# A hybrid decoder trunk on one core: order of work and of loads in the opening, and in group 2 of the second mixer

## The chip, the core and the metric

One core of a Trainium2 chip runs the whole program in one launch. The metric is the device time of that core in microseconds (us); lower is better. In the text PE is TensorE (matmuls; PEld its weight loads), DVE is VectorE, ACT is ScalarE, POOL is GpSimd, SP is SyncE, which here only issues loads. An engine runs its own instructions in order; engines wait for one another by semaphores.

## The reference

The trunk has two layers. Layer 0 is half-step SwiGLU, a GLA mixer, half-step SwiGLU; layer 1 is the same around a Mamba-2 (SSD) mixer. The input is 256 tokens of 1024 values in float32.

```python
def swiglu(h, w_gate, w_up, w_down):
    return (silu(h @ w_gate) * (h @ w_up)) @ w_down       # 1024 -> 2816 -> 1024

def ssd_mixer(h, ...):                                     # 8 groups of 256 channels
    z, xbc, dt = split(h @ w_in)
    xbc = silu(causal_conv4(xbc) + conv_b)                 # 4 taps along time
    xs, bm, cm = split(xbc)
    ... # chunked scan: scores cm.bm with decays, state carried over chunks, + d_skip * xs
    y = y * silu(z); y = rmsnorm over each group's 256 channels
    return y @ w_out

for i in range(2):
    x = x + 0.5 * rmsnorm(swiglu(rmsnorm(x, g[0]), ...), g[1])
    x = x + rmsnorm(mixer_i(rmsnorm(x, g[2])), g[3])
    x = x + 0.5 * rmsnorm(swiglu(rmsnorm(x, g[4]), ...), g[5])
```

## The kernel before

**Precision.** Each weight tile and each activation is split in two parts in float32r: a high part (a rounded copy) and a low part (the value minus the high part). Each product is three matmuls: high-high, high-low, low-high. So each weight tile that a load brings into `raw` costs ACT a copy (the high part, `hi` L538, or `gate_up_hi` L610 for a quarter of a gate and up pair) and DVE a subtraction (the low part, `lo` L1017, `gate_up_lo` L1099). PE waits for the low part. There are four weight slots in `raw` and `ws`: 0 and 1 hold gate and up of a unit in a SwiGLU, 2 and 3 hold two down tiles. In a mixer slot 0 is P1, 1 is P2, 2 is P3 and 3 is O (a quarter of the output weights, "out").

**A SwiGLU** runs over 11 units of 256 hidden columns, `u` = 0 to 10. For a unit PE sweeps over gate and up (48 matmuls of 512 columns, L1560, in four quarters by weight rows; a "half" of a unit's load is two quarters of both matrices). ACT takes silu of gate (`gate`, L615), DVE multiplies by up (`hidden`, L1105), PE transposes (`hidden_T`, L1571), ACT and DVE split the transposed values (`hT_high` L620, `hT_low` L1112), and PE multiplies them with the down tile (24 matmuls, L1581) after the next unit's sweep. In PE's order unit u's sweep is followed by the first half of down u-1 (12 matmuls), the transposes of unit u, the second half of down u-1, then the sweep of u+1. The code for one unit on ACT and on DVE is `body` in `ffn`. It begins with the high or low part of the down tile, then the next unit's first quarters, then silu or product of this unit.

**The opening** is the first SwiGLU's start. Unit 0's weights come in four quarter loads of each matrix, then SP issues unit 1 (two halves), down 0, down 1, unit 2 (two halves), down 2, and in a loop down u and unit u. A half of a unit's load waits until the low parts that free its place are made (`gu_lo`). POOL issues small parameter loads and the load of a row of gains for the first residual update (512 KB in the buffer `gpost`).

**The second mixer** (`ssd`) runs over 8 groups `g`, as a software pipeline: in step g PE projects group g (P1 gives x, P2 gives B and C, P3 gives z; 48 matmuls of 256 columns each), scans group g-1 and adds group g-2's output with quarter g-2 of the output weights. On DVE a group's projections pass `convolution(g, 0)` for x and `convolution(g, 2)` for B and C (each 2 tensor_scalar L1287 and 6 scalar_tensor_tensor L1290 of 256 columns), and a scanned group passes `norm` (some 13 operations on 2 columns, then two on 256 columns, L1374, which give `yn`). PE transposes x of group g-1 (`rows`, L1849) and `yn` of group g-2 (`transpose_rows`, L1839), and forms `scores` (L1858, L1861). ACT copies projections out of PSUM (`tiles_out`, L556), makes silu of z (`gate_silu`, L836), of the convolved features (`feature`, L842), the squares for the norm, and the transposed output (`transposed`, L877). POOL makes three scaled copies of the transposed x (`side_products`: `xw`, `xdt`, `dx`, L491, L494, L499), issues the spread of decay rows into `exps` and masks them (`causal`, L477). Steps 3 to 6 are one loop; steps 1, 2, 7 and later are written apart, with flags `first` (g is 1), `second` (g is 2), `ahead` (7) and `tail` (8).

## Time and profile before

| | us |
|---|---|
| median of 3 runs | 1115.28 (1114.52 to 1117.74) |
| the profiled execution, its own time | 1114.35 |
| its span in the profile, first to last instruction | 1112.6 |
| PE busy | 1094.2 (98%) |
| DVE, ACT, POOL busy | 727.4, 637.1, 54.9 |
| mean granted TensorE clock | 0.998 of full speed |

PE is busy nearly all the time, so time can come back only where it stands still or runs at a lower clock. In the timeline a row gives start, length, engine, line, operation, tiles and, in brackets, the idle time before it with the engine that ended it. Some rows merge several instructions (x2, x6): the length is then from the first start to the last end.

### The profile page before, as it was taken

What the parts mean: (1) busy time and instruction counts of PE and PEld (TensorE: products, weight loads), DVE (VectorE), ACT (ScalarE), POOL (GpSimd) and SP (SyncE); (2) the same over time, 40 slices, a digit from 0 to 9 for tenths busy, and PEclk for the clock granted to TensorE, in tenths of its full rate; (3) what the DMA queues carried; (4) which work ended last, traced back from release to release, by engine and by line L of the source; (5) the groups of instructions that cost most, each with busy time, mean ns of one, the idle gap of its engine ahead of it and who ended that gap; (6) DMA issues with size and microseconds to landing.
All of it is one profiled execution on the core that took longest, in us unless ns stands there. A gap on an engine that the chain in (4) does not pass through costs nothing.

```text
span 1112.6 us, 16272 instructions
## 1 busy us (share of the span) xinstructions
PE 1094.2 (98%) x5821; PEld 932.5 (84%) x5821; DVE 727.4 (65%) x1158; ACT 637.1 (57%) x994; POOL 54.9 (5%) x81
## 2 busy tenths in 40 slices
PE   9999999999999999999999999999999999999997
PEld 7788888899878888888888887899999977888886
DVE  5655555796686555558555546789999988545553
ACT  7544445685575444457544445686777787544443
POOL 3000000000000000000000000142111110000000
PEclk9999999999999999999999999999999999999999
DMA  9955653475357655554756546276544526656531
GB/s 276 319 167 179 211 166 115 132 228 176 128 154 246 224 167 173 181 196 157 239 169 210 185 125 200 88 237 224 174 151 151 165 107 223 228 168 223 164 102 38
DMA packets 162878, 199.26 MB, mean 179 GB/s; under 512 B 6372, under 2 KB 145856, under 8 KB 162832
## 3 DMA queue, kind: packets, MB, share of 16 engines
q1 hardware_dynamic: 160288, 190.86, 52.9%
q0 software_dynamic: 2384, 7.72, 2.2%
q8 instruction: 27, 0.44, 0.2%
q14 instruction: 19, 0.16, 0.0%
q10 hardware_dynamic: 160, 0.08, 0.0%
HBM read 197.56 MB, written 1.08 MB: 179 GB/s over the span
## 4 chain that ended last, share of the span: by engine, by line
PE 90%; DVE 5%; DMA 2%; ACT 2%; issue 1%; SPq 1%; DVEq 0%; ACTq 0%
PE ps L1560 42%; PE ps L1581 25%; PE ps L1616 10%; PE ps L1626 6%; PE ps L1571 2%; DMA raw<-in_ffn_w_down 1%; PE ps L1961 1%; DVE ws L1099 1%; DVE ws L1017 1%; DVE xres L1065 1%; DMA raw<-in_ffn_w_up 1%; PE ps L1733 1%; PE ps L1604 0%; ACT ws L538 0%; DVE xT L1089 0%
## 5 line engine op out<-in xcount | busy, mean ns | idle before, releaser
L1560 PE MATMUL ps<-ws,xT 128*128 128x512 f32 x2208 | 513.5, 390 | 2.7 <-DVE xT L1089 2.2
L1560 PEld LDWEIGHTS ps<-ws,xT 128*128 128x128 f32 x2208 | 412.0, 188 | 92.7 <-issue 4.8
L1581 PE MATMUL ps<-ws,hT 128*128 128x512 f32 x1344 | 330.7, 396 | 0.0
L1099 DVE TENSOR_TENSOR ws<-raw,ws 128x1024 fp32r<-128x1024 f32 x184 | 223.4, 1223 | 120.6 <-ACT ws L610 120.6
L1581 PEld LDWEIGHTS ps<-ws,hT 128*128 128x128 f32 x1344 | 248.5, 189 | 52.4 <-issue 2.0
L610 ACT ACTIVATE ws<-raw 128x1024 fp32r<-128x1024 f32 x184 | 193.2, 1061 | 151.0 <-PE ps L1560 143.3
L1017 DVE TENSOR_TENSOR ws<-raw,ws 128x2048 fp32r<-128x2048 f32 (+1 forms) x87 | 197.5, 2271 | 84.3 <-ACT ws L538 84.0
L538 ACT ACTIVATE ws<-raw 128x2048 fp32r<-128x2048 f32 x84 | 159.9, 1914 | 55.0 <-PE ps L1581 50.5
L1616 PE MATMUL ps<-xT,ws 128*128 128x256 f32 x960 | 119.0, 284 | 1.5 <-ACT feat L556 1.5
L1616 PEld LDWEIGHTS ps<-xT,ws 128*128 128x128 f32 x960 | 116.4, 192 | 2.2 <-DVE ws L1017 1.7
L1112 DVE TENSOR_TENSOR hT<-ps,hT 128x256 fp32r<-128x256 f32 x88 | 33.6, 419 | 84.6 <-ACT hT L620 84.4
L620 ACT ACTIVATE hT<-ps 128x256 fp32r<-128x256 f32 x88 | 29.5, 381 | 94.4 <-PE ps L1571 94.2
L1626 PE MATMUL ps<-ws,xT 128*128 128x256 f32 x576 | 73.6, 286 | 0.0
L1626 PEld LDWEIGHTS ps<-ws,xT 128*128 128x128 f32 x576 | 70.7, 191 | 1.0 <-issue 0.5
L615 ACT ACTIVATE fm<-ps,sm 128x256 f32<-128x256 f32 x88 | 41.2, 474 | 50.5 <-PE ps L1560 50.5
L1105 DVE SCALAR_TENSOR_TENSOR fm<-ps,sm,fm 128x256 f32<-128x256 f32 x88 | 41.8, 482 | 19.9 <-ACT fm L615 19.5
L1290 DVE SCALAR_TENSOR_TENSOR ca<-feat,pcol,ca 128x256 f32<-128x256 f32 x96 | 46.7, 552 | 0.0
L506 POOL DMA_DIRECT2D gpost<-in_norm_gain x5 | 2.7, 548 | 691.5 <-DVE scr L1047 691.5
L1089 DVE SCALAR_TENSOR_TENSOR xT<-ps,gcol,xT 128x128 fp32r<-128x128 f32 x96 | 26.6, 343 | 9.7 <-ACT xT L592 9.5
L592 ACT ACTIVATE xT<-ps,gcol 128x128 fp32r<-128x128 f32 x96 | 26.4, 379 | 11.2 <-PE ps L1604 11.2
L1571 PEld LDWEIGHTS ps<-ident,fm 128*128 128x128 f32 x176 | 22.2, 141 | 9.7 <-DVE fm L1105 3.4
L1571 PE MATMUL ps<-ident,fm 128*128 128x128 f32 x176 | 27.5, 276 | 2.8 <-DVE fm L1105 2.8
(225 smaller groups left out, 605.2 us busy)
## 6 DMA issues: line engine op xcount, KB each, us to landing
raw<-in_ffn_w_down SPq DMA_DIRECT2D x88, 512.0 KB, 4.3
raw<-in_ffn_w_gate SPq DMA_DIRECT2D x86, 512.0 KB, 4.0
raw<-in_ffn_w_up SPq DMA_DIRECT2D x86, 512.0 KB, 5.0
raw<-in_ssd_w_in SPq DMA_DIRECT2D x48, 512.0 KB, 4.7
raw<-in_gla_w_in SPq DMA_DIRECT2D x24, 512.0 KB, 4.9
raw<-in_ssd_w_out SPq DMA_DIRECT2D x16, 512.0 KB, 4.4
raw<-in_gla_w_out SPq DMA_DIRECT2D x8, 512.0 KB, 4.6
exps<-cs_rows POOLq DMA_DIRECT2D x8, 512.0 KB, 4.7
```

The costliest lines, as they stand in the source:

```text
L538: act.activation(ws[:, slot, 0, :], raw[:, slot, :], ACT.Copy).then_inc(hi_done[slot], 1)
L610: act.activation(ws[:, 0:2, 0, c], raw[:, 0:2, c], ACT.Copy).then_inc(gu_hi, 1)
L615: act.activation(fm[:, t, :], ps[:, bank + t, 0:UW], ACT.Silu, scale=RPRE[t]).then_inc(silu_g, 1)
L1017: return dve.tensor_tensor(ws[:, slot, 1, cols], raw[:, slot, cols], ws[:, slot, 0, cols].bitcast(F32), ALU.subtract)
L1099: dve.tensor_tensor(ws[:, 0:2, 1, c], raw[:, 0:2, c], ws[:, 0:2, 0, c].bitcast(F32), ALU.subtract).then_inc(gu_lo, 1)
L1105: dve.scalar_tensor_tensor(out=fm[:, 2 + t, :], in0=ps[:, bank + t, UW:2 * UW], scalar=RPRE[t], in1=fm[:, t, :], op0=ALU.mult, op1=ALU.mul ...
L1290: ins = dve.scalar_tensor_tensor(out=ca[:, c, :], in0=src, scalar=tap, in1=ca[:, c, :], op0=ALU.mult, op1=ALU.add)
L1560: mm = pe.matmul(ps[:, bank + t, :].rearrange("p (s n) -> p s n", s=2), xT[:, k, a, t * P:(t + 1) * P], ws[:, 0:2, b, k * UW:(k + 1) * UW] ...
L1571: mm = pe.transpose(ps[:, C + t, j * P:(j + 1) * P], fm[:, 2 + t, j * P:(j + 1) * P], ident[:, :])
L1581: mm = pe.matmul(ps[:, 2 * t + n, :], hT[:, par, j, a, t * P:(t + 1) * P], ws[:, slot, b, off:off + 512], start=(first and j + a + b == 0) ...
L1616: mm = pe.matmul(ps[:, banks + c, 0:T], ws[:, slot, a, off:off + P], xT[:, k, b, :], start=(k == 0 and a + b == 0), stop=(k == KD - 1 and ...
L1626: mm = pe.matmul(ps[:, banks + t, 0:UW], xT[:, k, a, t * P:(t + 1) * P], ws[:, slot if home is None else home, b, k * UW:(k + 1) * UW], st ...
```

## The change

In the opening (`ph == 0`), SP issues down 0 before unit 1, then unit 1, the first half of unit 2, down 1, the second half of unit 2, and down 2. Unit 3 is loaded before down 3. ACT and DVE work on down 1's parts after unit 1's silu, product and transposed parts, not before. POOL issues the gains row only when unit 2's second half has landed.

In the second mixer, DVE makes the high part of out quarter 0 (a copy, 128 x 2048) as well as the low part, both before step 1; ACT's copy for it is gone. The load of quarter 0 is issued before P1 and P2 of group 2. The low part of P2 for group 1 moves ahead of a convolution. In step 1 DVE makes the low part of P2 for group 2 ahead of `norm`. In step 2 (`second`): PE takes the rows of group 1 first and the transposes of group 0's `yn` between the two halves of P2; ACT takes silu of z and P3's high part ahead of the transposed output; the state is copied in the middle of group 2's first convolution; `convolution(2, 2)` moves behind the scan's output and the low part of P2 behind `norm`.

```diff
@@ SP, ffn: loads @@
+                    load_down(0)
                     if ph > 0:
-                        load_down(0)
                         load_down(1)
                     load_unit(1)
+                    load_gate_up(wg, 2 * UW, wu, 2 * UW, units + 2, 0)
                     if ph == 0:
-                        load_down(0)
                         load_down(1)
-                    load_unit(2)
+                    load_gate_up(wg, 2 * UW, wu, 2 * UW, units + 2, 1)
                     load_down(2)
                     for u in range(3, NF):
-                        load_down(u)
-                        load_unit(u)
+                        if ph == 0 and u == 3:
+                            load_unit(u)
+                            load_down(u)
+                        else:
...
@@ SP, mixer; POOL @@
+                    if ssd:
+                        load_out(0)
                     load_p12(2)
-                    load_out(0)
+                    if not ssd:
+                        load_out(0)
...
+            pool.wait_ge(gu_loaded[1], 64)
             pool.dma_start(gpost[:, :], gain_row(1)).then_inc(gpost_in, 16)
@@ ACT, ffn body (DVE's likewise with lo) @@
-                    hi(*down)
+                    opening = ph == 0 and not early
+                    if not opening:
+                        hi(*down)
...
                     hT_high(u + hiddens, 1, par)
+                    if opening:
+                        hi(*down)
@@ ACT, mixer body @@
+                    second = ssd and isinstance(g, int) and g == 2
-                    if scan and not tail and not (ssd and first):
+                    if scan and not tail and not (ssd and first) and not second:
                         gate_silu()
-                    if outp and (proj or not scan):
+                    if outp and (proj or not scan) and not second:
                         transposed(C)
...
+                    if second:
+                        gate_silu()
...
                             hi(SLOT_P3, g + n0[SLOT_P3])
-                        if ssd and isinstance(g, int) and g == 2:
+                        if second:
+                            transposed(C)
                             act.wait_ge(off_mm, G + 1)
...
                         for c in range(2):
                             feature(g, c)
-                        hi(*out_unit(g - 1, n, n0))
                         return
...
+                    if second:
+                        act.wait_ge(y_done, g)
+                        squares()
@@ DVE, ssd_start @@
+                lo(SLOT_P2, n0[SLOT_P2] + 1)
                 dve.wait_ge(p2_out, 2 * G + 2)
                 convolution(0, 2)
-                lo(SLOT_P2, n0[SLOT_P2] + 1)
+                slot, count = SLOT_O, n0[SLOT_O]
+                dve.wait_ge(loaded[slot], (count + 1) * 32)
+                dve.wait_ge(tile_mm[slot], count * 2)
+                dve.tensor_copy(ws[:, slot, 0, :], raw[:, slot, :]).then_inc(hi_done[slot], 1)
+                lo(slot, count)
@@ DVE, mixer body @@
-                        convolution(g, 0)
+                        convolution(g, 0, range(CONV // 2))
+                        if between is not None:
+                            between()
+                        convolution(g, 0, range(CONV // 2, CONV))
...
-                                x_convolved()
-                            state_copied()
+                                x_convolved(state_copied)
...
+                    if second:
+                        dve.wait_ge(p2_out, c0 + 2)
+                        convolution(g, 2)
                         norm(g, tail)
                     if proj and not ahead:
                         lo(SLOT_P2, g + n0[SLOT_P2] + 1)
+                    if first and ssd:
+                        norm(g, tail)
@@ PE, mixer body @@
-                        pe.wait_ge(p1_out, c0 + 2)
-                        if ssd:
+                        if second:
+                            feature_tiles(SLOT_P2, A, (0,), (p1_out, c0))
+                            pe.wait_ge(p3_out, c0)
+                            transpose_rows(C)
+                            feature_tiles(SLOT_P2, A, (1,), (p1_out, c0))
+                        elif ssd:
+                            pe.wait_ge(p1_out, c0 + 2)
                             feature_tiles(SLOT_P2, A)
```

The orders below name instructions by line, which shifts between the two programs. On ACT in the opening, from unit 1's last quarter on (L610 is a quarter's high part, L538 a down tile's, L615 silu, L620 the transposed high part), before:

```order
L610 ACTIVATE ws<-raw 128x2x512 [waits gu_mm,gu_loaded1]
L538 ACTIVATE ws<-raw 128x2048 [waits loaded2]
L620 ACTIVATE hT<-ps 128x2x128 [waits hT_mm] x2
L538 ACTIVATE ws<-raw 128x2048 [waits loaded3]
L610 ACTIVATE ws<-raw 128x2x512 [waits gu_read,gu_loaded0] x2
L615 ACTIVATE fm<-ps,sm 128x256 [waits gu_mm] x2
```

And after, where L618 is the quarter, L546 the down tile, L623 silu and L628 the transposed part:

```order
L618 ACTIVATE ws<-raw 128x2x512 [waits gu_mm,gu_loaded1]
L546 ACTIVATE ws<-raw 128x2048 [waits loaded2]
L628 ACTIVATE hT<-ps 128x2x128 [waits hT_mm] x2
L618 ACTIVATE ws<-raw 128x2x512 [waits gu_read,gu_loaded0] x2
L623 ACTIVATE fm<-ps,sm 128x256 [waits gu_mm] x2
L703 ACTIVATE pcol<-ps 128x256 [waits cols_T]
L705 ACTIVATE sw<-exps 128x8x16 [waits params_in]
L628 ACTIVATE hT<-ps 128x2x128 [waits hT_mm] x2
L546 ACTIVATE ws<-raw 128x2048 [waits loaded3]
```

Down 1's high part (the wait for `loaded3`) stood before unit 2's first quarters and unit 1's silu, and now stands behind both.

On DVE in the second mixer, from the last operation of step 1's scan to the low part of P3 in step 2 (L1290 with `ca` is the convolution, L1023 opens the norm, L1374 ends it, L1391 the transposed low part, L1017 a low part), before:

```order
L1491 TENSOR_TENSOR yn<-yn,zs 128x512 [waits zs_done,dve_step]
L1287 TENSOR_SCALAR ca<-feat,pcol 128x256 [waits feat_done,p1_out]
L1290 SCALAR_TENSOR_TENSOR ca<-feat,pcol,ca 128x256 [waits conv_step] x6
L1023 TENSOR_SCALAR sm<-sm 128x2 [waits y_sq]
...
L1374 TENSOR_SCALAR yn<-yn,sm 128x256 [waits y_done,dve_step]
L1017 TENSOR_TENSOR ws<-raw,ws 128x2048 [waits hi_done1]
L1287 TENSOR_SCALAR ca<-feat,pcol 128x256 [waits p2_out]
L1290 SCALAR_TENSOR_TENSOR ca<-feat,pcol,ca 128x256 [waits conv_step] x6
L1391 SCALAR_TENSOR_TENSOR hT<-ps,pcol,hT 128x256 [waits yT_hi] x2
L1017 TENSOR_TENSOR ws<-raw,ws 128x2048 [waits hi_done3]
L1429 TENSOR_TENSOR wm<-exps,scr 128x512 [waits decay_done,e_out]
```

And after (L1312 is the convolution, L1041 opens the norm, L1401 ends it, L1418 the transposed low part, L1035 a low part, L1457 the decayed scores `wm`):

```order
L1520 TENSOR_TENSOR yn<-yn,zs 128x512 [waits zs_done,dve_step]
L1309 TENSOR_SCALAR ca<-feat,pcol 128x256 [waits feat_done,p1_out]
L1312 SCALAR_TENSOR_TENSOR ca<-feat,pcol,ca 128x256 [waits conv_step] x6
L1035 TENSOR_TENSOR ws<-raw,ws 128x2048 [waits hi_done1]
L1041 TENSOR_SCALAR sm<-sm 128x2 [waits y_sq]
...
L1401 TENSOR_SCALAR yn<-yn,sm 128x256 [waits y_done,dve_step]
L1309 TENSOR_SCALAR ca<-feat,pcol 128x256 [waits p2_out]
L1312 SCALAR_TENSOR_TENSOR ca<-feat,pcol,ca 128x256 [waits conv_step] x6
L1418 SCALAR_TENSOR_TENSOR hT<-ps,pcol,hT 128x256 [waits yT_hi] x2
L1457 TENSOR_TENSOR wm<-exps,scr 128x512 [waits decay_done,e_out]
```

The low part of P2 (the wait for `hi_done1`) now precedes the norm, and the low part of out quarter 0 (`hi_done3`) is gone from step 2.

On PE in step 2, from the last matmuls of P1 (L1616) to the scores, before:

```order
L1616 MATMUL ps<-xT,ws 128x256 x23
L1839 MATMUL ps<-ident,yn 128x128 [waits yn_done,p3_out]
L1839 MATMUL ps<-ident,yn 128x128
L1839 MATMUL ps<-ident,yn 128x128 [waits yn_done]
L1839 MATMUL ps<-ident,yn 128x128
L1849 MATMUL ps<-ident,fm 128x128 [waits p3_out,feat_done]
L1849 MATMUL ps<-ident,fm 128x128 x3
L1616 MATMUL ps<-xT,ws 128x256 [waits p1_out,lo_done1]
L1616 MATMUL ps<-xT,ws 128x256 x47
L1858 MATMUL ps<-ident,fm 128x128 [waits feat_done,yT_lo]
```

And after (L1650 is a projection, L1884 the rows, L1874 the transposes of `yn`, L1893 the scores):

```order
L1650 MATMUL ps<-xT,ws 128x256 x23
L1884 MATMUL ps<-ident,fm 128x128 [waits p3_out,feat_done]
L1884 MATMUL ps<-ident,fm 128x128 x3
L1650 MATMUL ps<-xT,ws 128x256 [waits p1_out,lo_done1]
L1650 MATMUL ps<-xT,ws 128x256 x23
L1874 MATMUL ps<-ident,yn 128x128 [waits yn_done,p3_out]
L1874 MATMUL ps<-ident,yn 128x128
L1874 MATMUL ps<-ident,yn 128x128 [waits yn_done]
L1874 MATMUL ps<-ident,yn 128x128
L1650 MATMUL ps<-xT,ws 128x256 [waits p1_out]
L1650 MATMUL ps<-xT,ws 128x256 x23
L1893 MATMUL ps<-ident,fm 128x128 [waits feat_done,yT_lo]
```

The rows of group 1 come first, and the transposes of `yn` stand 24 matmuls later.

## Rows read from the trace of the kernel before

**Rows 1.** The page's first part: busy time, share and instructions of each engine.
```profile
PE 1094.2 (98%) x5821; PEld 932.5 (84%) x5821; DVE 727.4 (65%) x1158; ACT 637.1 (57%) x994; POOL 54.9 (5%) x81
```

**Rows 2.** Timeline of the opening: start, length in us, engine, line, operation, tiles.
```profile
12.04 1.06 ACT L610 ACTIVATE ws<-raw 128x1024 fp32r<-128x1024 f32 x1 [0.35 <-DMA raw<-in_ffn_w_up]
...
15.36 2.46 SPq L317 DMA_DIRECT2D raw<-in_ffn_w_down  x4
...
22.20 0.38 SPq L330 DMA_DIRECT2D raw<-in_ffn_w_gate  x1
...
26.41 1.91 ACT L538 ACTIVATE ws<-raw 128x2048 fp32r<-128x2048 f32 x1 [1.72 <-DMA raw<-in_ffn_w_down]
...
31.71 1.92 ACT L538 ACTIVATE ws<-raw 128x2048 fp32r<-128x2048 f32 x1 [2.84 <-DMA raw<-in_ffn_w_down]
...
32.89 3.01 PE L1581 MATMUL ps<-ws,hT 128*128 128x512 f32 x12
...
36.63 0.82 ACT L615 ACTIVATE fm<-ps,sm 128x256 f32<-128x256 f32 x2
...
38.14 0.87 DVE L1105 SCALAR_TENSOR_TENSOR fm<-ps,sm,fm 128x256 f32<-128x256 f32 x2
...
38.67 1.08 PE L1571 MATMUL ps<-ident,fm 128*128 128x128 f32 x4 [2.78 <-DVE fm L1105]
```

**Rows 3.** Chain of waits, 0 to 62 us: start, length, what; x is matmuls.
```profile
39.76 3.98 PE ps L1581 x12
43.74 10.88 PE ps L1560 x48
54.62 2.72 PE ps L1581 x12
...
60.53 1.59 PE ps L1560 x7
```

**Rows 4.** Stretches: length, busy time of each engine, granted clock, DMA share, GB/s.
```profile
36.00:45.00 9.00, 6.33 (x23) 5.06 (x24) 6.42 (x9) 5.81 (x10) 0.00 (x0) 0.81 0.92 325
```

**Rows 5.** Timeline of the second mixer, steps 1 and 2.
```profile
727.57 2.28 DVE L1429 TENSOR_TENSOR wm<-exps,scr 128x512 f32<-128x512 f32 x2 [1.43 <-ACT scr L906]
...
736.52 1.91 ACT L538 ACTIVATE ws<-raw 128x2048 fp32r<-128x2048 f32 x1
738.16 0.16 DVE L1023 TENSOR_SCALAR sm<-sm 128x2 f32<-128x2 f32 x1
...
741.11 2.28 DVE L1017 TENSOR_TENSOR ws<-raw,ws 128x2048 fp32r<-128x2048 f32 x1
...
743.65 5.99 PE L1616 MATMUL ps<-xT,ws 128*128 128x256 f32 x48 [1.51 <-ACT feat L556]
743.84 2.46 DVE L1290 SCALAR_TENSOR_TENSOR ca<-feat,pcol,ca 128x256 f32<-128x256 f32 x6
...
749.98 5.76 PE L1581 MATMUL ps<-ws,hT 128*128 128x512 f32 x24
...
758.21 0.41 DVE L1420 COPY scr<-ps 128x256 f32<-128x256 f32 x1
...
758.68 0.70 PE L1965 MATMUL ps<-scr,fm 128*128 128x256 f32 x2 [0.78 <-DVE scr L1420]
```

**Rows 6.** Timeline of step 8, VectorE: the end of the norm.
```profile
898.63 0.46 DVE L1361 SCALAR_TENSOR_TENSOR sm<-sm 128x2 f32<-128x2 f32 x1
899.13 1.72 DVE L1374 TENSOR_SCALAR yn<-yn,sm 128x256 f32<-128x256 f32 x2
```

**Rows 7.** The same stretch of step 8, GpSimd: the side products.
```profile
899.04 1.04 POOL L494 TENSOR_TENSOR xdt<-scr,dtv 128x512 f32<-128x512 f32 x1
900.04 1.28 POOL L499 TENSOR_TENSOR dx<-scr,hb 128x256 f32<-128x256 f32 x2
```

**Rows 8.** Timeline of step 3: the same convolution beside GpSimd's work.
```profile
775.55 4.08 DVE L1290 SCALAR_TENSOR_TENSOR ca<-feat,pcol,ca 128x256 f32<-128x256 f32 x6
```

**Rows 9.** Timeline before the second mixer: one-source operations on SBUF, 512 columns each.
```profile
695.93 0.88 DVE L1083 TENSOR_SCALAR scr<-xres,sm 128x512 f32<-128x512 f32 x2
```

More of the change, by code:

```diff
@@ L954, in body @@
                         act.activation(DUMMY, EPS_COL[1.0], ACT.Sqrt)
-                    if scan:
+                    if scan and not second:
                         if ssd:
@@ L1463, in body @@
                     if proj:
-                        if ssd and not ahead and not first:
+                        if ssd and not ahead and not first and not second:
                             dve.wait_ge(p2_out, c0 + 2)
@@ L1827, in body @@
                             pe.wait_ge(y_out, c0 - 2)
+                        second = ssd and isinstance(g, int) and g == 2
                         if scan:
@@ L1893, in add_output @@
                                 x_transposed(ph + 1, 0)
-                    if outp and proj:
+                    if outp and proj and not second:
                         pe.wait_ge(p3_out, c0)
```

23 lines of the change are left out of this document (15 added, 8 removed).

## The prediction, made before the changed kernel ran

> **What bounds the kernel now.** I read the page's first part, then the chain of waits, then the timelines around each place where PE stood still. PE is busy for 1094.2 of 1112.6 us [rows 1], and neither part of the change removes a matmul. So a gain can only be idle time of PE, or time at the lower clock. The reader should look in brackets on PE's rows: 2.78 us before the transposes at 38.67 [rows 2], 1.51 us before the projection at 743.65 and 0.78 us before the matmul at 758.68 [rows 5]. These are the places that the change touches.
>
> **Opening, what goes.** PE's transposes at 38.67 wait for DVE's product at 38.14, which waits for silu at 36.63. ACT had no reason of its own to be that late: it stood 2.84 us for down 1's load until 31.71, then made its high part, and unit 2's quarters, and only then silu [rows 2]. Undisturbed, PE goes from the start of a down tile's first 12 matmuls to the next sweep in 60.53 - 54.62 = 5.91 us [rows 3]. Here the first 12 start at 32.89 [rows 2], so the next sweep could start at 38.8; in the chain's reckoning, which counts a little later than the rows, I take 38.95. It starts at 43.74 [rows 3]. The difference is 4.8 us: 2.78 idle, and the rest is a slower PE afterwards. The 12 matmuls at 39.76 take 3.98 us against 2.72 at 54.62 [rows 3], and the four transposes take 1.08 us [rows 2] against (5.91 - 2 x 2.72) = 0.47. The granted clock over 36 to 45 us is 0.81 [rows 4], so part of this stretch ran at 1.2 instead of 2.4 GHz, after PE had stood still. Without the idle time I expect no fall there.
>
> **Opening, what is late next.** In the new order ACT meets: down 0's high part, unit 0's transposed part, unit 2's first two quarters, silu of unit 1, the transposed part, down 1's high part. Down 0 is issued at about 6 us, behind unit 0's loads, and no longer at 15.36; ACT waited for it 1.72 us until 26.41 [rows 2], so that wait goes too. Unit 2's first half is still issued at 22.20 [rows 2], since DVE's low parts decide that, but down 1 (1 MB) and the gains row (0.5 MB) are no longer in front. Over 36 to 45 us the DMA engines move 325 GB/s [rows 4]. At that rate 1.5 MB are 4.6 us: its work on ACT started at 34.5 before (silu's 36.63 less two quarters of 1.06 [rows 2]), so it can start by 30. Two quarters take it to 32.1, or 33. Silu is wanted from the end of unit 1's sweep on, a little before 32.89, and its product by 35.7, when PE comes to the transposes; silu and product together take about 1.4 us [rows 2]. So there are 1 to 1.5 us to spare. Down 1's parts then start at 36.8: 1.92 on ACT [rows 2], 2.28 on DVE [rows 5], done by 41.1, wanted near 52. Unit 2's third quarter follows at about 42.3 and is wanted at 38.95 + 5.44 = 44.4. Unit 3's second half is issued near 43.5 and used near 48.5, wanted around 50. All hidden; if the first of these covers were gone, each us by which silu starts after 34.2 would cost one. I take -4.8, and keep -3.5 and -5.2 as ends (the lower one adds part of ACT's earlier waits; PE's own idle before 14 us is outside the change).
>
> **Second mixer, step 1.** DVE gains a copy of 128 x 2048. The trace has no such copy. A one-source operation of 512 columns on SBUF takes 0.44 [rows 9], which gives 4 x 0.44 = 1.76; with the 0.16 of a 2-column one [rows 5] as a fixed part it is 0.16 + 4 x 0.28 = 1.3. The two-source one of 2048 takes 2.28 [rows 5], the upper end. I take 1.3, by the nearest rows of one source. It starts after the convolution, near 723.9 (727.57 less 1.43 idle and a low part of 2.28 [rows 5]); 1.3 and a low part of 2.28 end at 727.5, which is where `wm` starts now, at 727.57 [rows 5]. So it costs 0 at my value. At 2.28 `wm` starts 0.9 later, and PE, which has no wait for it today, loses at most that; I count 0.6. By the Trainium skill ("VectorE: DVE Perf Modes", section Mode 2x_2P) an fp32 copy with source and destination in SBUF delivers two results per cycle, which makes about 1.2 us of it as an estimate; then step 1 costs nothing. If it ran at one result per cycle, as a two-source operation does, the estimate is 2.3 us and the sum 0.6 higher. No row here shows the copy. ACT saves the copy's 1.9 us behind 740.6.
>
> **Second mixer, step 2.** What goes: the 1.51 us at 743.65, because PE no longer wants both x features of group 2 behind `yn`, and ACT takes them first; and the 0.78 us at 758.68, because the state copy, now at 758.21, comes about 4 us earlier in DVE's order (a low part 2.28 and half a convolution before it go). What comes: the norm of group 1. Today it runs from 738.16 to 741.11, 2.95 us [rows 5], when GpSimd is idle. Now DVE first makes P2's low part, which needs ACT's high part, done at 736.52 + 1.91 = 738.43. So the low part runs to 740.7 and the norm would end at 743.65. But PE's rows and ACT's copy of x also come earlier (P1 of group 2 ends at 743.65 - 1.51 - 2 x 0.47 = 741.2, rows to 741.7, copy to 742.4), and with it GpSimd's side products start at 742.5, in the middle of the norm.
> How they meet is shown in step 8. There a 2-column operation that takes 0.16 alone (the one at 738.16 does [rows 5]) takes 0.46, and the two of 256 columns take 1.72 together [rows 6], beside `xdt` at 899.04 and `dx` at 900.04 [rows 7]: VectorE gets one operation in per operation of GpSimd. At 742.5 the norm has six operations to go, and GpSimd has four (0.6, 1.04 and 1.28 for two [rows 7]), to 745.4. So `yn` is ready at about 745.0 and 745.6, not 743.65. PE has rows to 741.7 and half of P2 (24 matmuls at 5.99 / 48 [rows 5]) to 744.6, waits about 1 us, transposes, and ends the other half at 748.8. The convolution of B and C starts at 745.5; its 2.46 + 0.5 [rows 5] meet GpSimd's masking, as in step 3 where the same six take 4.08 [rows 8], 1.6 more. I take 0.9 more: done at 749.3. Silu of both, 0.9, ends at 750.2, and the scores wait for it: PE loses 1.4 more. Then output quarter 0 starts at 750.8, against 749.98 now [rows 5]. The 0.8 us lost there and the 0.78 saved at the state copy cancel. DVE comes to step 3 about 0.3 us later than now, which its own waits in each step take up. I take -0.1 for the mixer, between -2.8 (neither collision) and +1.8 (both at full price: 1.7 more on the convolution than assumed, or the copy at 2.28).
>
> **The sum.** -4.8 - 0.1 = -4.9 us. The profiled execution took 1114.35, so 1109.45. The median of the runs, 1115.28, is 0.9 above that execution; by it the sum is 1110.4. I name 1109.8.
>
> **Rivals.** (a) *No collision in step 2.* If ACT's copy of x comes late enough for the norm to pass, PE goes 741.2, rows, P2 with `yn`'s transposes inside, scores, and starts quarter 0 at 748.4, 1.6 earlier than now. With the state copy's 0.78 and small change that is -2.8: 1114.35 - 4.8 - 2.8 = 1106.8. For it: the row of step 8 shows two or three collisions only. Against: GpSimd's 2.9 us are fixed to PE's rows. Chance 0.14.
> (b) *Step 1 and 2 both lose.* Quarter 0's load now runs in front of the decay rows and delays them, the copy is slow, and `wm` and the convolution come late: 0.6 in step 1, and 0.9 more in step 2. 1109.45 + 1.5 = 1111.0. Chance 0.14.
> (c) *Silu of unit 1 is still late.* Unit 2's first half lands with little gain, since the parameter loads and down 0 take the rate that down 1 left. If its quarters start at 34.5 as now, silu starts at 36.6 as now and DVE, without down 1's low part ahead, makes the product about 0.6 earlier: PE still waits about 2.2 us, and I count half of the 4.8 as kept at most. Time 1109.45 + 2.4 = 1111.9. Chance 0.07.
> (d) *Slower: down 0 in the way of the first unit.* It is issued while unit 0's last quarter is still on its way (that quarter is used at 12.04 [rows 2]). If the DMA engines serve it beside or ahead of that quarter, PE stands still in the first sweep. Down 1's 1 MB took from 26.41 to 31.71, 5.3 us [rows 2], as the highest price of such a load. 5.3 idle, plus a fall of the clock as after 38.67, (3.98 - 2.72) + 0.6 = 1.9: 1109.45 + 7.2 = 1116.6. It decides from 3.0 us of delay on, where 3.0 + 1.9 use up the 4.9. Against it: the four down loads issued from 15.36 on landed one after the other, 26.41 and 31.71, behind what was issued before them, so one queue is served in its order. Chance 0.03.
>
> **How the numbers follow.** The forecast, 1108.6 to 1110.6, has 0.62. A measurement of this kernel tells about 0.3%, 3.3 us, from no change: faster than that means under 1111.9. Forecast, (a) and (b) lie there, and half of (c): 0.90 less a little for the spread of the medians, 0.88. Same is 0.09: the rest of (c), and mild forms of (d). Slower is 0.03. The range reaches from between (a) and the forecast, 1107.2, to 1111.9.
>
> **What would show it.** Right: no PE idle near 36 to 39 us, granted clock 1.0 from 24 to 60 us, unit 2's sweep at about 39; no idle before the second state matmul of step 2; a PE wait for `yn` inside P2 of about 1 us and one before the scores of about 1.4, with the norm's last operations stretched to 0.5 and more beside GpSimd's. Wrong: silu of unit 1 after 35 us; a PE wait before 15 us that is longer than now; `yn` ready by 744 (then (a)); P3 of group 2 starting (now right behind 758.68) before 752.7 or after 755.7; the copy at over 2 us.

## The result, and the profile after

The changed kernel takes 1115.95 us (median of 20 runs, 1114.73 to 1117.99), the kernel before 1114.28 (20 runs, 1112.27 to 1117.74). The ratio is 1.0017, 95% interval 1.0009 to 1.0024. The forecast was 1109.8, in a range of 1107.2 to 1111.9, so it is wrong in size and in sign. The profiled execution after took 1115.49 us, its span is 1113.8; before they were 1114.35 and 1112.6. The page's first part after, to be read beside [rows 1]:

```profile
PE 1094.5 (98%) x5821; PEld 932.9 (84%) x5821; DVE 730.5 (66%) x1159; ACT 634.9 (57%) x993; POOL 53.0 (5%) x81
```

PE's busy time is the same. So idle time that left one place came back in another. The opening did what it should. Its timeline after (start, length, engine, line, operation, tiles, idle time before):

```profile
32.90 0.97 DVE L1123 SCALAR_TENSOR_TENSOR fm<-ps,sm,fm 128x256 f32<-128x256 f32 x2
...
35.67 0.60 PE L1605 MATMUL ps<-ident,fm 128*128 128x128 f32 x4
36.02 3.02 PE L1615 MATMUL ps<-ws,hT 128*128 128x512 f32 x12
...
38.88 11.04 PE L1594 MATMUL ps<-ws,xT 128*128 128x512 f32 x48
```

And two stretches after (length, busy time of PE, its weight loads, DVE, ACT, POOL, granted clock, DMA share, GB/s):

```profile
36.00:45.00 9.00, 9.00 (x43) 7.43 (x41) 7.18 (x7) 7.59 (x8) 0.00 (x0) 1.00 0.48 154
715.00:726.00 11.00, 7.87 (x53) 7.67 (x53) 4.97 (x11) 5.87 (x15) 3.28 (x4) 0.84 1.04 328
```

The product is made at 32.90, not 38.14; PE has no idle time before the transposes; the sweep of unit 2 starts at 38.88 where it started at 43.58 in the timeline (43.74 in the chain, [rows 3]), 4.7 earlier; the granted clock is 1.00 from 36 to 45, where it was 0.81 [rows 4]. The second stretch shows the bill: 3.1 us of idle PE, and a clock of 0.84.

I follow PE through the second mixer by five marks: A, where it starts the long stretch of P1 and P2 matmuls behind the decay sums (711.39 before, 706.82 after); B, P2 of step 1 behind the scores; C, P1 of step 1; D, output quarter 0 in step 2; E, P3 of group 2 behind it. Each number is the start of that group on PE in the profile, counted from A of the same profile, so that the opening drops out.

| | B | C | D | E |
|---|---|---|---|---|
| before | 15.38 | 20.79 | 38.59 | 47.64 |
| after | 20.25 | 25.97 | 45.25 | 53.28 |

After is 4.87 behind by B, 0.31 more by C, 1.48 more by D, and wins 1.02 back by E: 5.64 against a gain of 4.57 at A. Nearly all of it is lost between A and B. There the profile before reads:

```profile
712.00 0.32 ACTq L799 DMA_DIRECT2D cs_rows<-dx  x1
...
713.74 1.05 POOL L513 DMA_DIRECT2D exps<-cs_rows  x2 [21.27 <-DMA cs_rows<-dx]
...
718.25 1.09 POOL L477 TENSOR_SCALAR_AFFINE_SELECT exps<-exps 128x1024 f32<-128x1024 f32 x1 [3.45 <-DMA exps<-cs_rows]
```

And after, where the store of the decay rows (`cs_rows`), their spread (`exps`), the mask, ACT's decays, its copy of a projection (`feat`) and PE stand in a row:

```profile
707.01 0.82 SPq L317 DMA_DIRECT2D raw<-in_ssd_w_out  x2
707.43 0.33 ACTq L811 DMA_DIRECT2D cs_rows<-dx  x1
...
711.14 1.05 POOL L521 DMA_DIRECT2D exps<-cs_rows  x2 [23.34 <-DMA cs_rows<-dx]
...
718.98 1.09 POOL L485 TENSOR_SCALAR_AFFINE_SELECT exps<-exps 128x1024 f32<-128x1024 f32 x1 [6.79 <-DMA exps<-cs_rows]
720.10 1.28 ACT L781 ACTIVATE exps<-exps,dtv 128x128 f32<-128x128 f32 x4 [6.87 <-POOL exps L485]
721.28 0.36 ACT L798 ACTIVATE feat<-ps 128x256 f32<-128x256 f32 x1
721.70 4.63 PE L1650 MATMUL ps<-xT,ws 128*128 128x256 f32 x24 [3.13 <-ACT feat L798]
```

Out quarter 0's load (1 MB) is issued 0.42 us before the small store. From the store's issue to the spread's issue it takes 3.71, before 1.74; from there to the mask 7.84, before 4.51. ACT stands in its queue behind the decays with the copy that frees PE's bank, so PE waits 3.13 us and then runs 24 matmuls in 4.63 instead of 3.1.

Step 1 and step 2 after. `wm` (L1457) starts 0.98 behind B, where it started 0.80 behind it before (727.57, [rows 5]), and in step 2 the norm (L1048 to L1401) meets GpSimd:

```profile
724.59 1.22 DVE L1358 CAST ws<-raw 128x2048 fp32r<-128x2048 f32 x1
...
728.05 2.55 DVE L1457 TENSOR_TENSOR wm<-exps,scr 128x512 f32<-128x512 f32 x2
...
742.93 0.63 POOL L499 TENSOR_TENSOR xw<-scr,dtv 128x256 f32<-128x256 f32 x1 [8.18 <-ACT scr L899]
...
744.62 0.54 DVE L1050 SCALAR_TENSOR_TENSOR sm<-sm 128x2 f32<-128x2 f32 x1
745.19 2.33 DVE L1401 TENSOR_SCALAR yn<-yn,sm 128x256 f32<-128x256 f32 x2
...
746.00 0.41 PE L1874 MATMUL ps<-ident,yn 128*128 128x128 f32 x2 [0.91 <-DVE yn L1401]
747.58 0.44 PE L1874 MATMUL ps<-ident,yn 128*128 128x128 f32 x2 [1.17 <-DVE yn L1401]
...
751.57 0.30 PE L1893 MATMUL ps<-ident,fm 128*128 128x128 f32 x1 [0.69 <-ACT fm L854]
752.07 5.74 PE L1615 MATMUL ps<-ws,hT 128*128 128x512 f32 x24
```

### The profile page after: what moved, and what is told of

The parts are those of the page before. It is cut to its first block and busy times, and to the rows that moved or that the text cites. A ratio compares the mean times of both kernels' runs of the same rounds, so it can differ in the third digit from the quotient of the medians.

```text
span 1113.8 us, 16272 instructions
## 1 busy us (share of the span) xinstructions
PE 1094.5 (98%) x5821; PEld 932.9 (84%) x5821; DVE 730.5 (66%) x1159; ACT 634.9 (57%) x993; POOL 53.0 (5%) x81
## 5 line engine op out<-in xcount | busy, mean ns | idle before, releaser
L618 ACT ACTIVATE ws<-raw 128x1024 fp32r<-128x1024 f32 x184 | 193.3, 1061 | 151.3 <-PE ps L1594 142.9
L1035 DVE TENSOR_TENSOR ws<-raw,ws 128x2048 fp32r<-128x2048 f32 (+1 forms) x87 | 197.1, 2267 | 79.5 <-ACT ws L546 79.0
L546 ACT ACTIVATE ws<-raw 128x2048 fp32r<-128x2048 f32 x83 | 158.0, 1914 | 49.0 <-PE ps L1615 49.0
L1650 PE MATMUL ps<-xT,ws 128*128 128x256 f32 x960 | 121.0, 286 | 3.3 <-ACT feat L798 3.1
L1650 PEld LDWEIGHTS ps<-xT,ws 128*128 128x128 f32 x960 | 118.0, 194 | 4.2 <-ACT feat L798 3.3
L628 ACT ACTIVATE hT<-ps 128x256 fp32r<-128x256 f32 x88 | 29.4, 381 | 95.1 <-PE ps L1605 95.1
L623 ACT ACTIVATE fm<-ps,sm 128x256 f32<-128x256 f32 x88 | 41.2, 474 | 51.6 <-PE ps L1594 51.6
L1312 DVE SCALAR_TENSOR_TENSOR ca<-feat,pcol,ca 128x256 f32<-128x256 f32 x96 | 46.8, 553 | 0.0
L564 ACT ACTIVATE feat<-ps 128x256 f32<-128x256 f32 x28 | 10.6, 381 | 29.8 <-PE ps L1650 29.7
```

Source lines behind the costliest of these rows:

```text
L546: act.activation(ws[:, slot, 0, :], raw[:, slot, :], ACT.Copy).then_inc(hi_done[slot], 1)
L618: act.activation(ws[:, 0:2, 0, c], raw[:, 0:2, c], ACT.Copy).then_inc(gu_hi, 1)
L623: act.activation(fm[:, t, :], ps[:, bank + t, 0:UW], ACT.Silu, scale=RPRE[t]).then_inc(silu_g, 1)
L1035: return dve.tensor_tensor(ws[:, slot, 1, cols], raw[:, slot, cols], ws[:, slot, 0, cols].bitcast(F32), ALU.subtract)
L1312: ins = dve.scalar_tensor_tensor(out=ca[:, c, :], in0=src, scalar=tap, in1=ca[:, c, :], op0=ALU.mult, op1=ALU.add)
L1650: mm = pe.matmul(ps[:, banks + c, 0:T], ws[:, slot, a, off:off + P], xT[:, k, b, :], start=(k == 0 and a + b == 0), stop=(k == KD - 1 and ...
```

## The experiments

Ratios are to the kernel before, with their 95% interval. The marks of every profile:

| run | B | C | D | E | ratio |
|---|---|---|---|---|---|
| before | 15.38 | 20.79 | 38.59 | 47.64 | 1 |
| after | 20.25 | 25.97 | 45.25 | 53.28 | 1.0017 (1.0009 to 1.0024) |
| e1 opening only | 15.37 | 20.79 | 38.59 | 47.64 | 0.9967 (0.9956 to 0.9978) |
| e2 mixer only | 19.96 | 25.87 | 45.77 | 53.77 | 1.0038 (1.0025 to 1.0050) |
| e3 out load back | 16.18 | 29.92 | 50.88 | 58.91 | 1.0064 (1.0045 to 1.0083) |
| e4 out load alone | 20.29 | 25.72 | 46.56 | 54.60 | 1.0040 (1.0025 to 1.0055) |
| e7 ACT copies | 16.17 | 21.58 | 42.17 | 51.83 | 0.9991 (0.9982 to 1.0000) |
| e8 load held | 16.16 | 25.16 | 45.52 | 53.55 | 1.0013 (1.0001 to 1.0026) |
| e9 products held to the norm | 20.97 | 26.39 | 46.07 | 54.91 | 1.0035 (1.0025 to 1.0044) |
| e10 e8 and e9 | 16.18 | 23.87 | 44.78 | 53.93 | 1.0021 (1.0011 to 1.0031) |
| e11 held to the convolution | 19.53 | 25.90 | 41.96 | 49.96 | 0.9999 (0.9989 to 1.0008) |
| e12 e7, low part back | 15.38 | 20.79 | 41.39 | 52.26 | 0.9988 (0.9979 to 0.9998) |
| e13 copy late | 15.38 | 20.79 | 42.04 | 50.07 | 0.9992 (0.9982 to 1.0001) |
| e14 copy of 2 columns | 16.17 | 21.74 | 41.64 | 49.67 | 0.9995 (0.9984 to 1.0006) |
| e15 e12 and e11 | 15.38 | 20.79 | 39.18 | 47.22 | 0.9946 (0.9932 to 0.9959) |
| e16 e1 again | 15.38 | 20.79 | 40.76 | 48.82 | 0.9955 (0.9941 to 0.9968) |

One caution for the ratios: in the profiles PE also waited between 0 and 2.1 us for the first unit's weights in the first 15 us, with either opening, and that differs from execution to execution. The marks don't hold it, the ratios do.

**e1 and e2: the two halves of the change.** e1 is the diff's opening alone on the kernel before (SP's order of loads, the gains row's wait, ACT's and DVE's down parts behind the unit), e2 its mixer alone.

> The kernel before with the opening's part of the change alone. Theory Q (loads in front of the decay rows cost the mixer 4.6 us, the opening gave its 4.7): 4.7 us faster than before, ratio 0.9958, sweep of unit 2 at 38.9 us. Rival O (the opening's gain is lost again somewhere before the second mixer, since later stages absorb it): ratio 1.000. Theory C (collision of VectorE and GpSimd in step 2 costs all that the mixer costs) expects the same as Q here.

> The change without its opening part. Q and C: 5.9 us slower than before (4.6 before step 1, 0.5 in step 1, 0.6 to 0.8 in step 2), ratio 1.0052. Rival O: 1.2 to 1.7 us slower, ratio 1.0015.

Measured 0.9967 and 1.0038. The opening's gain is real and reaches the end: all marks of e1 are those of before. The theory that it is absorbed later falls. The mixer alone costs 4.2 us by the ratio, less than the 5.9 expected, which lies just outside the interval; by mark E its profile is 6.13 behind.

**e3 and e4: the load of out quarter 0.** e3 puts it back behind P2's in the changed kernel, e4 moves only it in the kernel before.

```diff
-                    if ssd:
-                        load_out(0)
                     load_p12(2)
-                    if not ssd:
-                        load_out(0)
+                    load_out(0)
```

> The whole change, but the load of output quarter 0 is issued behind P2 of group 2 again, as before. Q: the first decay rows land about 2.5 us after their issue is possible as before, PE's wait of 3.13 us for the copied feature and the half clock after it go, step 1's 0.5 us too: about 5 us faster than the changed kernel, ratio to before 0.9958 to 0.9967. C: no change against the changed kernel, ratio to before 1.0015, the PE wait stays. Rival P (it is the early load of P2 for group 2, issued as soon as the moved low part is made, that delays the decay rows): the wait stays at 2 us or more, ratio to before 1.000.

> The kernel before, with one thing changed: the load of output quarter 0 is issued in front of P1 and P2 of group 2 instead of behind. Q: the store of the decay sums takes 3.4 us instead of 1.5, and their spread 6 us or more instead of 4.5; PE waits for the copied feature for 1 to 3 us, ratio 1.0015 to 1.004. C: nothing, ratio 1.000. P: nothing or under 0.5 us, since P2's load is still late, ratio 1.000.

e4 confirms the mechanism. The ratio is at the upper end of what was expected and PE's wait, 3.31, above it. The load alone costs 4.91 us at mark B, as much as in the changed kernel (4.87). Its mask and its PE:

```profile
723.49 2.17 POOL L480 TENSOR_SCALAR_AFFINE_SELECT exps<-exps 128x1024 f32<-128x1024 f32 x2 [7.07 <-DMA exps<-cs_rows]
...
726.21 3.14 PE L1619 MATMUL ps<-xT,ws 128*128 128x256 f32 x24 [3.31 <-ACT feat L789]
```

The rival that blamed P2's earlier load falls with it, since that load stood late in e4, at 731.41. But e3 missed: I expected the time back, and it became the slowest of all. B is nearly right there (16.18), and then, in e3:

```profile
727.72 1.45 DVE L1355 CAST ws<-raw 128x2048 fp32r<-128x2048 f32 x1 [6.38 <-DMA raw<-in_ssd_w_out]
...
732.76 3.67 PE L1999 MATMUL ps<-xdt,wm 128*128 128x64 f32 x16 [6.13 <-DVE wm L1454]
```

VectorE's copy waits 6.38 us for the load, with `wm` behind it in VectorE's queue and PE behind `wm`. So the copy's place on VectorE forces the load's place on SP.

**e7, e8, e14: is it the copy, or where the load stands?** e7 gives the copy back to ACT (end of step 1) and puts load and low part back. e8 keeps the copy on VectorE and issues the load as late as the decay rows allow:

```diff
                     if ssd:
-                        load_out(0)
-                    load_p12(2)
+                        load_cols(SLOT_P1, w, 2 * UW + DI, used(2, SLOT_P1))
+                        sp.wait_ge(cs_loaded[1], 16)
+                        load_out(0)
+                        load_two(SLOT_P2, ...)
```

e14 is e8 with a copy of 2 columns instead of 2048, so quarter 0's high part is not made.

> After's kernel with the copy of out 0 back on ACT at the end of step 1, its low part in step 2 behind the transposed output, and its load behind P2 of group 2 again. Theory K (coupling: the load had to go in front of the decay rows only because VectorE copies early, and that order is what loses 4.6 us): the decay chain is on time, VectorE has no wait for out 0 before step 1, step 1 starts its P2 near 722.3 and loses nothing; in step 2 the collision of the norm with GpSimd stays (0.6 lost) and the low part of out 0, now 2.28 us behind the scores' features, makes quarter 0 start up to 1.4 later. Ratio to before 0.9975 (0.9955 to 0.999). Rival L (the step 1 order itself, with P2's low part ahead of the convolution, loses the time, whoever copies): PE still waits over 2 us before step 1, ratio above 1.000.

> After's kernel with out 0's load issued between P1 and P2 of group 2, and SP waiting before it until both first spreads of decay rows have landed. Theory K: decay rows on time (first mask near 713.8 as with the opening alone), out 0 issued near 715.3 and landed near 720.5, before VectorE comes to its copy at 721.3. No bank wait of 3 us on PE, no wait of 6 us on VectorE, clock 1.00 over 715 to 726. What is left of the loss is step 1 (0.5) and step 2 (0.6): -4.7 + 1.1 = -3.6 us, ratio 0.9968 (0.9955 to 0.998). Rival M (out 0 cannot be in time in either place, 1 MB lands later than 721.3 because P1 and the decay rows share the rate): VectorE waits for out 0 again, 2 us or more, ratio 0.9985 to 1.003.

> The kernel with out 0's load held behind the decay rows (run e8), with VectorE's copy of the high part cut from 2048 to 2 columns (the high part of quarter 0 is then not made). It measures the copy by itself where VectorE is the last to be ready in step 1. Theory D: wm starts 1.1 us earlier than 726.6, PE's waits before the state matmuls of step 1 (1.3 and 0.8 us) fall by 1.1 together, some 0.5 more comes back at the full clock: -1.1 to -1.6 us against e8, ratio 1.0000 (0.999 to 1.001). Rival (the load's landing at 722.8 alone decides, since the wait of 1.23 us for it stays): the copy's time is hidden, ratio 1.0013.

e7 returns 4.4 of the 5.2 us that the changed kernel had lost by C. Its ratio, 0.9991, is just outside the range named (0.9955 to 0.999), because step 2 lost more than expected: D is 3.6 behind that of before. PE waits there 1.26 us for ACT's copy of x, 1.61 for the features behind the convolution, which lies beside GpSimd's work as in e9 below, and 1.15 for out 0's low part. e8 missed what its theory expected. Its ratio is in rival M's range, but VectorE's wait for the load is 1.23 us and not M's 2 or more. Its decay rows were issued on time, and yet C is only 0.8 better than after:

```profile
722.82 1.23 DVE L1361 CAST ws<-raw 128x2048 fp32r<-128x2048 f32 x1 [1.23 <-DMA raw<-in_ssd_w_out]
...
724.51 3.08 POOL L505 TENSOR_TENSOR xdt<-scr,dtv 128x512 f32<-128x512 f32 x1
...
726.62 2.54 DVE L1460 TENSOR_TENSOR wm<-exps,scr 128x512 f32<-128x512 f32 x2
...
727.74 0.67 PE L1987 MATMUL ps<-xw,scr 128*128 128x256 f32 x2 [1.29 <-POOL xdt L505]
...
729.22 2.73 PE L2005 MATMUL ps<-xdt,wm 128*128 128x64 f32 x16 [0.81 <-DVE wm L1460]
```

`wm` starts at 19.44 behind A, against 16.18 before. With the copy cut, in e14, it starts at 723.79, 17.02 behind A:

```profile
721.36 0.17 DVE L1361 CAST ws<-raw 128x2 fp32r<-128x2 f32 x1 [0.17 <-DMA raw<-in_ssd_w_out]
...
723.79 2.53 DVE L1460 TENSOR_TENSOR wm<-exps,scr 128x512 f32<-128x512 f32 x2
```

`wm` is 2.42 earlier than in e8, counted from A: 1.06 of it is the copy, 1.06 is that the load happened to land earlier in this profile (its wait is 0.17, not 1.23), and the rest is a low part of 2.29 instead of 2.61. C comes 3.4 earlier, and by the ratios the run is 2.0 us faster; so neither is the copy's alone. In e8 the low part also lay beside GpSimd's `xdt`, which took 3.08 us (1.48 in e14), and PE's first wait, 1.29, is for `xdt`. The ratio is in the range of e14's theory, and the rival, by which the copy is hidden, expected 1.0013.

How much room VectorE has, e7 shows. There its second convolution in front of step 1 ends 14.4 behind A, against 12.5 before (e12 shows why), and `wm`, at 17.02, waits 2.60 for ACT. Out 0's low part (2.28) fits into that, as e14 shows, whose `wm` is at 17.02 too. The copy of 1.22 and the wait for the load don't fit. In the changed kernel this was hidden, because PE was already 4.9 late.

**e12: the low part of P2 beside the masks.** It is e7 with this low part behind the convolution again.

```diff
-                lo(SLOT_P2, n0[SLOT_P2] + 1)
                 dve.wait_ge(p2_out, 2 * G + 2)
                 convolution(0, 2)
+                lo(SLOT_P2, n0[SLOT_P2] + 1)
```

> The kernel with the copy of out 0 back on ACT and its load behind (run e7) with also P2's low part for group 1 back behind the convolution of B and C. Theory L (in its new place the low part lies beside GpSimd's two first masks and stretches them from 1.09 each to 4.1 together): masks at 1.1 each, ACT's decays start near 714.9 and not 716.6, step 1's P2 starts at 722.2 (722.96 in e7), its P1 at 727.6 (728.4). -0.7 us against e7: ratio 0.9985 (0.9975 to 0.9995). Rival: the masks stay long because of the row loads, ratio as e7, 0.9991.

First the mask in e7, then in e12:

```profile
713.51 4.13 POOL L482 TENSOR_SCALAR_AFFINE_SELECT exps<-exps 128x1024 f32<-128x1024 f32 x2 [3.31 <-DMA exps<-cs_rows]
```

```profile
713.83 1.09 POOL L482 TENSOR_SCALAR_AFFINE_SELECT exps<-exps 128x1024 f32<-128x1024 f32 x1 [3.55 <-DMA exps<-cs_rows]
```

As expected: 4.13 for two masks beside the low part, 1.09 each without it; B and C are those of before again, 0.8 earlier. This is a second, smaller loss of step 1, which a late decay row hid in the changed kernel. The ratio moved by 0.0003 only, inside its interval, and in e12's profile the gain is gone by E (52.26 against 51.83): quarter 0's 24 matmuls take 8.58 us there, 7.37 in e7 and 5.74 after.

**e9, e10, e11: the collision in step 2.** GpSimd's side products of step 2 wait for the norm (e9; e10 with e8's load), or for the whole convolution behind it (e11):

```diff
                 pool.wait_ge(tok_out, g - 1 + G + 1)
+                if g == 2:
+                    pool.wait_ge(yn_done, 2 * G + 2)      # e9, e10
+                    pool.wait_ge(conv_step, 32)           # e11 instead
```

> After's kernel with GpSimd's side products of group 2's step held until the norm's two results (yn) are made. Theory C (the norm is slow because VectorE's small operations stand beside GpSimd's): the norm takes 2.95 us again, yn is ready at 743.9 and 744.2, PE's waits of 0.91, 1.17 and 0.69 go, quarter 0 starts at 749.1 to 749.4 and not 752.07: -2.8 us against after, ratio to before 0.9992 (0.998 to 1.0003). Rival N (the norm is late for another reason, its inputs or the table loads): the waits stay within 0.3 us, ratio 1.0017 as after. Rival W (the held products come late and take the place of what was won): PE waits for xw or xdt before its state matmuls, or VectorE for dx, by over 1 us.

> After's kernel with both holds: out 0's load behind the decay rows, and the side products of step 2 behind the norm. If K and C both hold the parts add: -4.7 (opening) + 0.5 (step 1) + 0.6 - 2.8 (step 2) = -6.4 us, ratio 0.9943 (0.993 to 0.996), better than the opening alone (0.9967). If step 2's gain is taken up later by VectorE or by loads (P3 of group 3 at the same place in the program no earlier than with the opening alone), the ratio is 0.9965 or more.

> After's kernel with GpSimd's side products of step 2 held until VectorE's whole second convolution (B and C of group 1) is done, not only the norm as in the run before. Theory C, widened (whatever VectorE runs beside these four operations is stretched, the norm if they start at 742.9, the convolution if they start at 745.3): the norm takes 2.95 us and the convolution 3.0, its result is there near 747.4, silu 748.3, PE has no wait in step 2 before quarter 0, which starts at 749.1 to 749.5 and not 752.07. Total -2.7 us against after: ratio to before 0.9993 (0.9982 to 1.0005). Rival W (held products come late): GpSimd's 3.3 us then start near 747.4 and end at 751, PE wants them at 755; a wait for xw or xdt over 0.5 us would speak for it.

In e9 the norm took 2.95 us again and PE's waits for `yn` went, as expected, but the time did not come back: at 1.0035, outside its range, e9 is slower than the changed kernel. GpSimd now started ahead of the convolution's six operations:

```profile
744.48 0.62 DVE L1403 TENSOR_SCALAR yn<-yn,sm 128x256 f32<-128x256 f32 x2
...
745.25 0.61 POOL L501 TENSOR_TENSOR xw<-scr,dtv 128x256 f32<-128x256 f32 x1 [9.87 <-DVE yn L1403]
...
745.93 5.22 DVE L1314 SCALAR_TENSOR_TENSOR ca<-feat,pcol,ca 128x256 f32<-128x256 f32 x6
...
752.30 0.45 PE L1895 MATMUL ps<-ident,fm 128*128 128x128 f32 x1 [3.14 <-ACT fm L856]
```

The six operations take 5.22 instead of 2.46, and the wait moved to the scores, 3.14. e10 showed the same, so its hoped-for sum of gains missed. In e11, with GpSimd behind both:

```profile
744.75 2.46 DVE L1314 SCALAR_TENSOR_TENSOR ca<-feat,pcol,ca 128x256 f32<-128x256 f32 x6
...
747.35 0.61 POOL L501 TENSOR_TENSOR xw<-scr,dtv 128x256 f32<-128x256 f32 x1 [12.61 <-DVE ca L1314]
...
748.86 5.71 PE L1617 MATMUL ps<-ws,hT 128*128 128x512 f32 x24
```

No PE wait is left from C to D, and C to E takes 24.06 us, against 27.31 after and 26.85 before. The ratio fell from 1.0017 to 0.9999, 2.0 us by the two medians' ratios. It was expected at 0.9993 (0.9982 to 1.0005). The collision, not the new order, is what cost in step 2.

**e13: a late copy on VectorE.** Loads and step 1 as before, the copy behind P1's low part in step 1, the low part in step 2, the side products held as in e11.

```diff
                         lo(SLOT_P1, g + n0[SLOT_P1] + 1)
+                    if first and ssd:
+                        dve.wait_ge(loaded[slot], (count + 1) * 32)
+                        dve.tensor_copy(ws[:, slot, 0, :], raw[:, slot, :])...
```

> A try for a better kernel: opening as after, step 1 and loads as before, step 2's order as after, GpSimd's side products of step 2 held behind the convolution, VectorE makes the copy of out 0 in step 1 behind P1's low part (so its load can stay behind P2), the low part in step 2 behind the transposed output. Theory D (VectorE has no room between the start of step 1 and quarter 0: with the opening alone it is busy 35.1 of the 38 us from 722 to 760, so each us given to it comes back on PE): decays and step 1 on time (P1 at 727.6), no wait of PE for x features and none for yn, but quarter 0 waits for its low part until 746.5 to 747 against 745.4 with the opening alone; P3 of group 2 at 754.8 to 755.3 against 754.47. Ratio 0.9971 (0.996 to 0.9983), no better than the opening alone. Rival F (ACT's copy was the bottleneck and its removal is the gain): quarter 0 at 744 or earlier, ratio below 0.9955.

```profile
731.90 1.23 DVE L1486 CAST ws<-raw 128x2048 fp32r<-128x2048 f32 x1 [1.93 <-DMA raw<-in_ssd_w_out]
...
734.34 7.47 PE L1651 MATMUL ps<-xT,ws 128*128 128x256 f32 x48 [2.02 <-issue]
...
750.35 5.74 PE L1616 MATMUL ps<-ws,hT 128*128 128x512 f32 x24 [1.36 <-DVE ws L1034]
```

C is on time, D is 3.45 late. VectorE waits 1.93 for the load. PE then stands still for 2.02 within P1 of step 1, while the scan's last operations on VectorE stand behind the copy; the profile names no releaser, so that link is read from the order of time. Quarter 0 waits 1.36 for its low part. The theory that VectorE has no room had the sign, and the time is above its range (0.9992 against at most 0.9983), since I had not counted on the load being late there. Rival F, by which ACT's copy was the bottleneck, is refuted.

**e15 and e16: the best of it.** e15 is e12 with e11's hold: the new opening, loads and step 1 and ACT's copy as before, step 2 in the new order with the side products behind the convolution. e16 is e1 again, beside it on the same chip.

> Opening as after; loads, step 1 and ACT's copy of out 0 as before; step 2's order as after, with its low part of out 0 behind the transposed output, and GpSimd's side products of step 2 held until the second convolution is done. Theory C with D (the collision is gone, but VectorE's work up to quarter 0, with the low part of out 0 in it, is as long as PE's): P1 of step 1 at 727.7, PE still waits 1.3 for x features (ACT's copy is in front of them), norm and convolution in 2.95 and 3.0, quarter 0 at 745.4 to 745.9 against 745.4 with the opening alone, and PE saves the 0.8 before the second state matmul: ratio 0.0003 to 0.0008 below that of the opening alone, so about 0.996 (0.995 to 0.9975). Rival (a) of the prediction, the order wins as soon as nothing is stretched: quarter 0 at 743.9 or earlier, 1.5 to 2.8 us below the opening alone, ratio 0.9945 or less. Rival N (nothing to win, VectorE is late for quarter 0 by 1 us or more): ratio equal to the opening alone or above.

> The opening of after with the mixer of before, a second time, as the pair of e15 on the same chip: 0.9967 as before (0.9958 to 0.9975). The profile: sweep of unit 2 at 38.9, P3 of group 2 at 754.5, apart from what the loads of the first unit take in the first 15 us, where PE waited between 0 and 2.1 us in the profiles so far, with either opening.

e15 takes 1109.68 us (5 runs, 1109.64 to 1110.22), e16 1110.71 (5 runs, 1110.50 to 1111.02), beside 1115.39 for before on that chip. No run of e15 is as slow as any of e16, so e15 beats before and the opening alone; after was not run beside it, but its ratio is 0.0071 higher. Both ratios are a little below the ranges named (0.995 and 0.9958 at the lowest), so it is their difference, 0.0009, that counts: 0.0003 to 0.0008 was expected. In e15's step 2 neither norm nor convolution is stretched:

```profile
738.82 3.11 PE L1647 MATMUL ps<-xT,ws 128*128 128x256 f32 x24 [1.26 <-ACT feat L563]
...
740.11 2.46 DVE L1312 SCALAR_TENSOR_TENSOR ca<-feat,pcol,ca 128x256 f32<-128x256 f32 x6
...
742.72 0.61 POOL L498 TENSOR_TENSOR xw<-scr,dtv 128x256 f32<-128x256 f32 x1 [12.75 <-DVE ca L1312]
...
746.53 5.74 PE L1612 MATMUL ps<-ws,hT 128*128 128x512 f32 x24 [0.74 <-DVE ws L1035]
```

D is 39.18, 0.6 behind the undisturbed 38.59 of e1 (P2 waits 1.26 for ACT's copy of x, quarter 0 waits 0.74 for the low part), E 0.42 ahead of it. So against e1's profile the new order wins 0.4, against e16's 1.6, since e16's profile had a collision of its own, though it is the same program as e1 (see the last section). Which of the two the other runs of e16 resemble is not recorded, so how the 1.0 us between the medians divides stays open. Rival (a)'s 2.8 us are not there without VectorE's early copy. With it they are: e11, where norm and convolution are not stretched, takes 24.06 from C to E against 26.85 before, 2.79 less.

## Why the prediction was wrong

**Opening, what goes and what is late next.** Right, in time and in mechanism: -4.7 at the sweep of unit 2 against -4.8, the clock at 1.00, silu done by 33.4, down 1's parts from 36.63 (36.8 forecast) with no PE wait. In whole runs it is 0.9967 and 0.9955, 3.7 and 5.0 us. Rivals (c) and (d) did not happen.

**Second mixer, step 1.** This step failed. It priced VectorE's copy rightly: 1.22 us measured, 1.3 taken, and the 1.2 worked out from the Trainium skill ("VectorE: DVE Perf Modes", Mode 2x_2P) agrees with the trace. But it let the copy start 12.5 behind A, where the convolution ended before. It started 17.8 behind A. What the step put at nothing is the load that this copy pulled forward. That load stood in rival (b) as "delays the decay rows", with 0.6 and 0.9 us for everything; the changed kernel lost 4.87 by mark B, and the load alone costs 4.91 (e4). The mistake was in reading: I took the copy's engine time as the cost of the move, and went through the queues that its load was moved past only for a remark. The chain store, spread, mask, decays, bank copy, PE stood in the trace before with its own waits (3.45 us of POOL for `exps`), and I did not follow it to PE. That `wm` itself came only 0.18 later behind B is no proof of the step's sum: with the decay rows late, PE was late as well. The step also left out that P2's low part, in its new place, stretches GpSimd's masks: 0.8 us at B by e7 and e12.

The experiments also say what stood behind that: with the copy in front of step 1 there was no good place for this load among those tried. In front it delays the decay rows (e4), behind it stalls VectorE by 6.38 us (e3), in between C is still 4.4 late (e8; 0.8 of it is there by B and comes from the masks). The loss by C goes when the copy is given back to ACT (e7, and wholly in e12), or when VectorE makes it later (e13), where PE then waits in step 1 and at quarter 0.

**Second mixer, step 2.** The mechanism was right, and shown by e11: a small operation of VectorE takes 0.54 beside GpSimd's against 0.46 expected, the two of 256 columns 2.33 against 1.72. So the second half of `yn` was ready 1.3 us later behind C than I had it. PE's waits came to 0.91 + 1.17 + 0.69 where I had 1.0 and 1.4, and the wait at the state copy went, as forecast. From C to E the changed kernel loses 0.46, where I had -0.1. A small mis-size.

**The sum.** Predicted -4.8 - 0.1. Traced: -4.6 at A, +4.9 from A to B, +0.3 to C, +0.5 to E, +1.1 in all, as the span (+1.2). The term of A to B is 4.9 of the 6.0 missed. P3 of group 2 at 760.10 is far beyond the 755.7 that was named as a sign of being wrong. By the prediction's own band of 3.3 us a result 1.7 slower is "same", which had 0.09. That was filled from the opening, with (c) and mild forms of (d), though the mixer moved a 1 MB load ahead of a 32 KB transfer that a whole chain hangs on. The faster side was added up too low besides: forecast, (a), (b) and half of (c) make 0.935, not 0.90.

## What to carry to other kernels

When an edit gives work to another engine earlier, the load of its data moves too, and it must be priced past every transfer it overtakes, small ones above all, down to the engine that waits at the end. When undoing one part makes things worse, ask which other part had made it necessary, and undo both. Work of GpSimd beside a busy VectorE is best placed behind the whole run of operations that PE waits for; put behind the first of them only, it stretches the next.
